# Second expert's products between the first expert's turns, at the start of an expert stage

## What is computed

```
xt = h.reshape(T, D)
logits = xt @ w_router + b_router
top_v, top_e = lax.top_k(logits, TOP_K)          # TOP_K = 4, 32 experts
weights = softmax(top_v)
# for each expert e, on the tokens that chose it:
hcat = x[tok] @ w1[e] + b1[e]                     # 1024 x 2048
x_glu = minimum(hcat[:, ::2], 7.0)
x_lin = clip(hcat[:, 1::2], -7.0, 7.0)
act = x_glu * sigmoid(1.702 * x_glu) * (x_lin + 1.0)
y = act @ w2[e] + b2[e]                           # 1024 x 1024
out[token] = sum over its 4 experts of y * weight
```

## Time and profile before

| | us |
|---|---|
| median of three runs | 2597.3 |
| lowest, highest | 2596.09, 2599.88 |
| the profiled execution | 2600.78 |
| its span, first to last instruction | 2599.0 |
| TensorE, VectorE, ScalarE called busy | 2566.8, 1339.4, 783.3 |

### The profile page before, as it was taken

The page is one execution under the profiler, slowest core; times in us unless marked ns, Lnnn a source line. Parts: engine busy times, 40 slices in busy tenths (PEclk is TensorE's granted clock), DMA queues, the critical chain, the costliest instruction groups (busy, mean ns, idle before and its releaser), DMA issues.

```text
span 2599.0 us, 39525 instructions
## 1 busy us (share of the span) xinstructions
PE 2566.8 (99%) x16005; PEld 1894.5 (73%) x16005; DVE 1339.4 (52%) x1733; ACT 783.3 (30%) x1318; POOL 76.2 (3%) x99
## 2 busy tenths in 40 slices
PE   9999999999999999999999999999999999999998
PEld 9989898999999899999999988833333333333333
DVE  6866785687788668656863684312112122112112
ACT  4414441443344144423423363122121121121111
POOL 0000200000000020000001000000000000000000
PEclk9999999999999999999999999999999999999999
DMA  6685443456655843345563636799999999999998
GB/s 230 212 294 170 138 151 146 146 178 225 229 192 183 298 168 130 130 146 169 178 213 113 232 123 253 294 375 426 427 427 428 428 427 428 428 428 427 427 428 363
DMA packets 264380, 702.27 MB, mean 270 GB/s; under 512 B 12996, under 2 KB 155280, under 8 KB 214992
## 3 DMA queue, kind: packets, MB, share of 16 engines
q1 hardware_dynamic: 249616, 650.03, 65.0%
q0 software_dynamic: 12480, 46.90, 4.9%
q10 hardware_dynamic: 2176, 3.83, 0.5%
HBM read 696.47 MB, written 6.60 MB: 271 GB/s over the span
## 4 chain that ended last, share of the span: by engine, by line
PE 83%; DMA 10%; SPq 4%; DVE 1%; ACT 1%; issue 1%; DVEq 0%; ACTq 0%
PE acc L1950 12%; PE acc L1148 6%; PE mix L1152 6%; PE acc L1150 6%; PE acc L1965 6%; PE acc L1221 5%; PE mix L1142 3%; PE acc L1237 3%; PE acc L1120 3%; PE acc L1094 3%; PE acc L1171 2%; PE acc L1688 2%; SPq L980 2%; DMA spare<-in_w 2%; DMA ring<-in_w 2%; PE acc L1179 2%
## 5 line engine op out<-in xcount | busy, mean ns | idle before, releaser
L1148 PE MATMUL acc<-branch_parts,area_parts 128*128 128x256 f32 x1176 | 344.1, 293 | 0.1
L1152 PE MATMUL mix<-big_parts,zz_parts 128*128 128x256 f32 x1176 | 332.8, 283 | 0.0
L1150 PE MATMUL acc<-area_parts,ring_parts 128*128 128x256 f32 x1176 | 332.5, 283 | 0.0
L2608 DVE TENSOR_TENSOR ring_parts<-ring,area_parts 128x1792 fp32r<-128x1792 f32 (+2 forms) x139 | 262.5, 1889 | 97.2 <-ACT area_parts L2110 60.5
L3470 DVE COPY zz<-acc 128x512 f32<-128x512 f32 x32 | 22.1, 692 | 545.2 <-PE acc L1950 545.2
L1148 PEld LDWEIGHTS acc<-branch_parts,area_parts 128*128 128x128 f32 x1176 | 225.0, 191 | 9.2 <-DVE big_parts L2608 0.6
L1150 PEld LDWEIGHTS acc<-area_parts,ring_parts 128*128 128x128 f32 x1176 | 225.1, 191 | 0.2
L1152 PEld LDWEIGHTS mix<-big_parts,zz_parts 128*128 128x128 f32 x1176 | 225.0, 191 | 0.0
L2110 ACT ACTIVATE area_parts<-ring 128x1792 fp32r<-128x1792 f32 (+1 forms) x116 | 189.6, 1634 | 16.4 <-DMA ring<-in_ffn_up 12.1
L2701 DVE SCALAR_TENSOR_TENSOR zz_parts<-area_parts,ring_parts 128x1792 fp32r<-128x1792 f32 x84 | 170.1, 2025 | 6.3
L2102 ACT ACTIVATE area<-acc 128x512 f32<-128x512 f32 (+2 forms) x67 | 32.0, 477 | 346.7 <-PE acc L1881 334.5
(11 more groups left out here) (586 smaller groups left out, 4915.3 us busy)
## 6 DMA issues: line engine op xcount, KB each, us to landing
ring<-in_ffn_up SPq DMA_DIRECT2D x86, 1024.0 KB, 5.0
big<-in_w SPq DMA_DIRECT2D x77, 1024.0 KB, 25.7
ring<-in_w SPq DMA_DIRECT2D x76, 1024.0 KB, 25.7
ring<-in_w_in SPq DMA_DIRECT2D x72, 1024.0 KB, 7.0
area<-in_w SPq DMA_DIRECT2D x58, 1024.0 KB, 25.9
spare<-in_w SPq DMA_DIRECT2D x38, 1024.0 KB, 25.5
area<-in_w_ada POOLq DMA_DIRECT2D x24, 1024.0 KB, 8.2
ring<-in_ffn_down SPq DMA_DIRECT2D x28, 768.0 KB, 4.8
```

Of the source, the lines that this page charges most:

```text
L1148: pe.matmul(abank(a, b)[:, ts], wg[:, b, k, c * P:c * P + P], xg[:, k, :], start=c == 0 and k == 0, stop=False, skip_group_check=True)
L1150: pe.matmul(abank(a, b)[:, ts], wl[:, k, c0:c0 + P], xl[:, k, :], start=False, stop=k == K - 1, skip_group_check=True)
L1152: mm = pe.matmul(kbank(a, b)[:, ts], wk[:, b, k, c * P:c * P + P], xk[:, k, :], start=False, stop=k == K - 1, skip_group_check=True)
L2608: return v.tensor_tensor(out, a, b, op)
```

## The change

It is made in three places. `turn` takes the bank to turn into. TensorE waits for both copies of the first expert's banks, does the second expert's first product, turns the first half into `Y_BANK`, does two more products, turns the second half into `X_BANK`, does the fourth, waits until VectorE has read both turned banks, and goes on with the gather for expert 3. Two b2 matmuls move from behind the turns to the five that close the part. VectorE's first pass reads its turned rows from the two other banks. The diff is whole.

```diff
-            def turn(it, a):
+            def turn(it, a, bank=None):
 
                 pe.wait_ge(h_copied[a], it + 1)
+                bank = H_BANK[a] if bank is None else bank
                 h = h_slot[:, a, :].rearrange("p (f n two) -> p n two f", n=2, two=2)
                 for odd in range(2):
                     for n in range(2):
                         c0 = (2 * odd + n) * P
-                        mm = pe.transpose(H_BANK[a][:, c0:c0 + P], h[:, n, odd, :], ident)
+                        mm = pe.transpose(bank[:, c0:c0 + P], h[:, n, odd, :], ident)
                 mm.then_inc(h_turned, 1)
...
+                def up_next(a, b):
+                    for k in range(a, b):
+                        pe.wait_ge(x_slot_ready, (first + 1) * DC + (k + 1))
+                        up_unit(q, k, DC + k)
+
...
                 gather_turn(first + 2)
                 up_first(6, 8)
                 add_b2(q, 0, 1)
-                turn(first, 0)
-                turn(first, 1)
-                add_b2(q, 1, 3)
-                slots_free(first + 1)
-                up(8, 0, 4)
+                for a in range(2):
+                    pe.wait_ge(h_copied[a], first + 1)
+                up_next(0, 1)
+                turn(first, 0, Y_BANK)
+                up_next(1, 3)
+                pe.wait_ge(x_slot_ready, (first + 1) * DC + DC)
+                turn(first, 1, X_BANK)
+                up_next(3, 4)
+                pe.wait_ge(h_read, (first + 1) * 2 + 1)
                 gather(first + 3)
                 up(8, 4, 6)
                 gather_turn(first + 3)
                 up(8, 6, 8)
                 down_between(1, 16)
-                add_b2(q, 3, DC)
+                add_b2(q, 1, DC)
...
-            def swiglu(it, e, up_units, down_units):
+            def swiglu(it, e, up_units, down_units, banks=H_BANK):
...
-                    tt(glu[:, a, :].rearrange("p (n s) -> p n s", s=C_SLOT), H_BANK[a].rearrange("p (n s) -> p n s", s=C_SLOT),
+                    tt(glu[:, a, :].rearrange("p (n s) -> p n s", s=C_SLOT), banks[a].rearrange("p (n s) -> p n s", s=C_SLOT),
...
-                swiglu(first, slice(0, 1), used + 9, used + 1)
+                swiglu(first, slice(0, 1), used + 9, used + 1, banks=(Y_BANK, X_BANK))
```

## The result

The changed kernel takes 2604.6 us (12 runs, 2602.31 to 2613.03) against 2597.71 (12 runs, 2596.09 to 2600.31): ratio 1.0026, 95% interval 1.0018 to 1.0034, 6.9 us slower. That is outside the range of 2595.3 to 2602.0 and on the slower side of 0.2%.

The account below looks back on a forecast made before the run. The weight stream was taken to bound the expert stage. Its shift, 0.1 run dry plus 1.0 restart plus 0.5 at the 17th transfer, 1.6 us, on the median 2597.3 gave 2598.9; range 2595.3 to 2602.0.

Parts of the forecast that it names:

- The earlier first product: Second expert's first product starts 2.0 us earlier, and with it the 1st weight transfer, counted from SyncE's issue at 1710.41.
- The turns: Two turns between the second expert's products cost 0.83 us each, leaving TensorE 0.35 us ahead after four units.
- The wait for the selectors: Before the gather for expert 3, TensorE idles 2.5 us for VectorE's selectors; transfers 5 and on are issued 2.2 later.
- The bias terms: Two terms moved behind the second expert's products add 0.97 us; TensorE is 3.2 us later from the 13th transfer.
- Rival (C): The stall drops TensorE's clock from 2.4 to 1.2 GHz; four units at half rate add 6.9 us, 2604.2; chance 0.04.
- (4): Step on the two bias terms moved back to make seven: 0.97 us more TensorE work, at 0.48 us each.
- What the stream passes on: Of TensorE's 3.2 us delay the weight stream passes on 1.6: 0.1 run dry, 1.0 restart, 0.5 at the 17th transfer.
- a spare of 3.2 at the 17th transfer: The 17th weight transfer lands 8.4 us after issue, a lone one 5.2, so 3.2 us of delay is just met.
- Rival (D): The weight stream runs dry several times and takes TensorE's whole delay or a little more: 2600.5 and up; chance 0.10.
- (A): Rival: the weight stream absorbs the stall, its queue never empties; 0 to 0.8 us faster, 2596.9; chance 0.18.
- (B): Rival: selectors come in time, no stall before the gather, the whole 2.0 us early start stays: 2595.3; chance 0.06.

Follow-up runs that it names:

- stall filled: The changed kernel with five unneeded matmuls of 256 columns in front of the gather for expert 3, while TensorE waits: 2604.09 us, ratio 1.0025.
- early selectors: The changed kernel with VectorE making expert 2's selectors before the bias adds, in the first expert's pass alone: 2601.21 us, ratio 1.0011.
- gather and bias terms later: The changed kernel with expert 3's gather two units later and the last six bias terms behind the down products of experts 4 and 5: 2596.6 us, ratio 0.9996.
- bias terms only: The kernel before with only the two bias terms moved to the other five, so seven stand in a row: 2600.85 us, ratio 1.0009.
- delay late: The kernel before with six unneeded matmuls behind the five bias terms, delaying TensorE from the 13th transfer on: 2601.76 us, ratio 1.0015.
- delay early: The kernel before with six unneeded matmuls ahead of the gather for expert 3: 2600.68 us, ratio 1.0008.

## Why the prediction failed, point by point

**The earlier first product** held: 1.75 us instead of 2.0. The row shows a wait of 0.45 behind the bias term that the sum had as 0.3. **The turns** held: the 4th transfer came 0.1 early where 0.35 was forecast, the rest being the same 0.25.

**The wait for the selectors** held: 2.36 us for a forecast 2.5. With the clock kept up ("stall filled") the 5th transfer is 2.5 late, forecast 2.2. **The bias terms** held as work: 0.9 (early selectors, 5th to 17th transfer) against 0.97. TensorE's delay without the clock is 2.5 + 0.9 = 3.4 us, forecast 3.2.

**The clock was the first step that failed**, in two places. Rival (C), with a chance of 0.04, said that the stall lets the clock fall. It did, and cost 1.7 us, not 6.9: the gather and the very start of the next unit ran at half rate, not four units. The reason that I gave against it was a single execution in which the clock stayed up beside an idle time of the same length; the trace of "gather and bias terms later" shows the same idle time of 2.5 us with the clock down behind it. One execution was too little to rest a chance of 0.04 on. The Trainium skill, "TensorE: Matmul & The Clock Gate", section "Loop structure matters more than you think", had warned that a long wait between matmuls lets the engine go cold. The stall of 2.36 us behaved so in the changed kernel's trace, with a granted clock of 0.50 behind it. The second place was in no rival: seven matmuls of 32 rows in a row, with no idle time, cost another 1.7 us. In this stretch seven in a row show the fall in three of four traces (changed, stall filled, bias terms only; not in early selectors), five in a row in none of the seven that have them, before included. Split into two and five, the same work runs at clock 1.00 in two traces, and the 17th transfer comes 1.3 us earlier than with seven in a row. That favours the run of narrow matmuls as what matters, but does not prove it: the seven too were without a fall in one trace and in six of the 11 timed runs of "bias terms only", so it takes something more than their number, which no run here isolates. The failed step is (4), where I costed the two moved matmuls by their duration alone.

**What the stream passes on was the second.** I took 1.6 us of 3.2, by a spare of 3.2 at the 17th transfer computed as its time to landing less that of a lone one. "Delay late" puts 2.8 us on exactly those transfers and the stream is 2.7 behind; "delay early" puts 2.9 on the 5th and on, and 2.1 arrive. The failed step is to read a landing time less that of a lone transfer as time to spare. The landing time counted the slowest engine, which already lagged: the signals of the 16 engines come 4.4 to 5.2 us after the issue of the 1st transfer and 5.5 to 8.4 after that of the 17th, but the middle one at 4.8 and 6.0, only 1.3 apart. And the loss is not confined to a queue that has run dry: in "delay late" the stream runs at 322 GB/s for 8 us with a DMA share of 0.96. In the changed kernel 6.7 us on TensorE became 6.6 at the end. Rival (D), that the stream takes TensorE's whole delay, was right on this and had 0.10.

**The sum by what was measured:** early start less turns -0.1; stall 2.6 (2.36 of idle time and the gather's start behind it); first fall 1.7; two bias terms 0.9; second fall 1.7; together 6.8 us of delay on TensorE, 6.7 by the 17th transfer, 6.6 of it passed on to the stream, against 6.9 in the medians. Without the two falls the forecast's mechanism gives 3.4 at most, 2601.1, inside the range. Rivals (A) and (B) are out: the stall was there and was not absorbed. That the medians follow the traces' falls one by one is not shown: the early selectors are 2.9 us slower by the median with a trace that shows no fall, and with the seven split as well the loss is gone. The granted clocks of the timed runs fit a fall in most of the early selectors' executions and not in the other's: 2 of 11 and 7 of 11 are at 1.000. They don't show it, since the early selectors' profiled execution is itself below 1.000, at 0.999, with no fall in this stretch but one behind the last matmul.

**On the change itself:** an earlier start of the second expert is worth nothing by itself. What it gains at the 1st transfer must also hold at the 13th to 17th, where TensorE's order leaves the stream nothing to spare. The bias terms alone far later, without the early start, gain nothing either (0.2 us behind). The traces show a gain held only with both (1.4 us ahead, 0.9 after 400 us), and the timed runs can't tell that version from before.

## What to carry to other kernels

Before moving a producer behind more work, follow the consumer engine's whole queue past it: here VectorE's selectors stood behind the two adds, and nothing in the edited lines named them. Where a transfer stream is the bound, look at how many transfers are in flight just behind the change: with few, count most or all of a delay of TensorE as a delay of the kernel (2.1 of 2.9 us and 2.7 of 2.8 here), and read GB/s rather than the DMA share. Give an idle time of 1.3 to 2.5 us, and a long row of matmuls that use a fraction of the rows, a chance of a clock fall on top of their own length, 1.7 us each here, unless several executions show that the clock stays.

## What the hardware showed beyond this

- A row of seven matmuls on 32 of 128 rows (3.3 us, no idle time) was followed by a granted clock of 0.50 in three traces of four, and without the early start by none in six timed runs of 11. A row of five (2.4 us) was not in any of seven traces.
- An idle time of 2.5 us in the dense part was followed by half clock in one execution and by full clock in another; one of 1.30 us right behind narrow matmuls was followed by half clock, one of 1.04 us behind turns ("bias terms only") was not.
- The weight stream at 322 GB/s shows a DMA share of 0.96, at 426 GB/s one of 1.01.
- Where a pass of TensorE's loop was written out, six instruction fetches and a loss of 0.5 us of the weight stream stand in the same 235 us, in both kernels that have it.
